# Turning the probabilities of the last attention with products instead of the transpose mode

## The reference, cut to what matters

```
s = einsum('bqghd,bkgd->bghqk', q, k) * scale
p = masked_softmax(s, mask)
o = einsum('bghqk,bkgd->bqghd', p, v)
out = g0 * o_cmp + g1 * o_slc + g2 * o_win
```

## Time and profile before

| | us |
|---|---|
| median of three timed executions | 2057.7 |
| fastest and slowest of them | 2040.02, 2061.91 |
| profiled execution, device time | 2035.77 |
| its span | 2034.0 |
| TensorE matmul busy | 1925.6 (95%) |
| VectorE busy | 1185.1 (58%) |
| ScalarE busy | 683.2 (34%) |
| last attention, first to last TensorE instruction | about 1669.7 to 1888.5 |

### The profile page before, as it was taken

The page is one execution under the profiler, slowest core; times in us unless marked ns, Lnnn a source line. Parts: engine busy times, 40 slices in busy tenths (PEclk is TensorE's granted clock), DMA queues, the critical chain, the costliest instruction groups (busy, mean ns, idle before and its releaser), DMA issues.

```text
span 2034.0 us, 25450 instructions
## 1 busy us (share of the span) xinstructions
PE 1925.6 (95%) x9553; PEld 1581.9 (78%) x9553; DVE 1185.1 (58%) x2640; ACT 683.2 (34%) x1170; POOL 101.9 (5%) x198
## 2 busy tenths in 40 slices
PE   3999999999999999989999999999999899999778
PEld 3886768988888887778888988888888776676767
DVE  5775564776476665664444487647757944533442
ACT  3323563523232342232223352323233334533121
POOL 0001110001000001100000000100110000000000
PEclk9998999999999999999999999999999999955779
DMA  8344331335334437622222243633442231010411
GB/s 333 125 145 140 100 114 63 124 126 173 138 109 127 154 125 243 221 93 104 83 90 81 79 161 128 206 128 136 135 176 83 90 118 42 1 65 1 177 39 62
DMA packets 44405, 246.05 MB, mean 121 GB/s; under 512 B 6080, under 2 KB 6304, under 8 KB 25728
## 3 DMA queue, kind: packets, MB, share of 16 engines
q1 hardware_dynamic: 23200, 153.26, 21.1%
q0 software_dynamic: 21088, 91.21, 13.4%
HBM read 229.23 MB, written 15.22 MB: 120 GB/s over the span
## 4 chain that ended last, share of the span: by engine, by line
PE 84%; DVE 9%; DMA 3%; ACT 2%; issue 1%; SPq 0%; DVEq 0%; ACTq 0%
PE ps L457 64%; PE ps L628 6%; PE ps L649 5%; PE ps L638 3%; DVE w_lo L1308 3%; DMA ada_raw<-in_ada 2%; PE ps L767 1%; ACT w_hi L923 1%; DMA bv_g<-in_bv_g 1%; DVE ada_raw L1336 1%; PE ps L879 1%; PE ps L891 1%; DVE pre L1429 1%; PE ps L714 1%; PE ps L892 0%
## 5 line engine op out<-in xcount | busy, mean ns | idle before, releaser
L1308 DVE TENSOR_TENSOR w_lo<-w_raw,w_hi 128x2048 fp32r<-128x2048 f32 x136 | 311.6, 2291 | 149.0 <-ACT w_hi L923 148.7
L923 ACT ACTIVATE w_hi<-w_raw 128x2048 fp32r<-128x2048 f32 x136 | 260.1, 1913 | 396.5 <-PE ps L457 374.0
L457 PE MATMUL ps<-h_hi,w_hi 128*128 128x512 f32 (+1 forms) x1008 | 380.9, 378 | 11.8 <-issue 4.6
L457 PE MATMUL ps<-h_lo,w_hi 128*128 128x512 f32 (+1 forms) x1008 | 375.1, 372 | 0.0
L457 PE MATMUL ps<-h_hi,w_lo 128*128 128x512 f32 (+1 forms) x1008 | 374.6, 372 | 0.0
L457 PEld LDWEIGHTS ps<-h_hi,w_hi 128*128 128x128 f32 x1008 | 192.5, 191 | 45.5 <-issue 6.2
L457 PEld LDWEIGHTS ps<-h_hi,w_lo 128*128 128x128 f32 x1008 | 192.2, 191 | 32.9
L457 PEld LDWEIGHTS ps<-h_lo,w_hi 128*128 128x128 f32 x1008 | 192.4, 191 | 30.7
L457 PE MATMUL ps<-hid_hi,w_hi 128*128 128x512 f32 (+1 forms) x576 | 211.3, 367 | 0.0
L457 PE MATMUL ps<-hid_hi,w_lo 128*128 128x512 f32 (+1 forms) x576 | 210.6, 366 | 0.0
L457 PE MATMUL ps<-hid_lo,w_hi 128*128 128x512 f32 (+1 forms) x576 | 210.5, 366 | 0.0
(11 more groups left out here) (359 smaller groups left out, 2755.5 us busy)
## 6 DMA issues: line engine op xcount, KB each, us to landing
w_raw<-in_slabs SPq DMA_DIRECT2D x136, 1024.0 KB, 4.8
ada_raw<-in_ada POOLq DMA_DIRECT2D x108, 512.0 KB, 4.5
s_tables<-s_tab POOLq DMA_DIRECT2D x4, 2692.0 KB, 9.2
s_t<-s_tables POOLq DMA_DIRECT2D x4, 2692.0 KB, 9.6
ada_first<-in_ada SPq DMA_DIRECT2D x4, 1536.0 KB, 18.3
a_bias<-in_a_bias POOLq DMA_DIRECT2D x16, 256.0 KB, 3.0
xT<-in_xT SPq DMA_DIRECT2D x1, 2048.0 KB, 20.0
s_toeplitz<-KTp POOLq DMA_DIRECT2D x32, 64.0 KB, 3.5
```

Of the source, the lines that this page charges most:

```text
L457: last = mm(o, l, r, start=start and n == 0, stop=stop and n == 2)
L923: A(w_hi[s][:], w_raw[:, s, :], ACT.Copy).then_inc(sem("hi_done"), 1)
L1308: tt(w_lo[s][:], w_raw[:, s, :], w_hi[s][:].bitcast(F32), ALU.subtract).then_inc(sem("lo_done"), 1)
```

## The change

On h_p, the last attention's probabilities, line 638 no longer uses the transpose mode: it issues an ordinary float32 product with the tile as stationary and the identity as moving operand, into the same place. The first attention keeps the transpose mode. Waits, signals, banks and order stay as they are.

```
                         for j in range(0, n, P):
                             w = min(P, n)
-                            last = nc.tensor.transpose(b[0:w, j:j + P], pt[:, u % 4, j:j + w], ident[:])
+                            if pre == "h":
+                                last = mm(b[0:w, j:j + P], pt[:, u % 4, j:j + w], ident[:], start=True, stop=True)
+                            else:
+                                last = nc.tensor.transpose(b[0:w, j:j + P], pt[:, u % 4, j:j + w], ident[:])
                         last.then_inc(sem(pre + "t_full"), 1)
```

## The result

The changed kernel took 2071.49 us (median of 4 executions, 2063.91 to 2088.23) against 2056.77 us (2040.02 to 2061.91) before. The ratio is 1.0125, with a 95% interval of 1.0072 to 1.0177: slower by 1.2%, where 2012 us was forecast. The profiled execution took 2067.79 us, with a span of 2066.0; its counterpart before had 2035.77 and 2034.0. Each later ratio is to executions of the kernel before from the same series (medians 2045.75 to 2057.16 us), and leaves out executions more than 1.5% above the fastest of their kernel, while a median holds all of them.

A forecast was written before the change was run, and what follows sets the result against it. TensorE was taken to bound the kernel, at half clock late in the last attention. With the clock held, +13.4 - 39.5 - 1.8 = -27.9 us made 2035.8 into 2007.9, plus 4 us gave 2012; range 1992 to 2062.

The forecast's parts named there:

- What bounds the stage: Last attention: the chain of waits lies on TensorE alone, 23% of it on line 638, at either clock.
- Price of a large tile: Line 638, full clock: a group's first tile costs 0.15 us more, each further tile 0.111 us.
- The lower bound: Line 638: longer turning eats its 2.2 us wait for ScalarE, leaving 0.8 us per 12 units; chance 0.06.
- Price of a small tile: Line 638, 32-key tiles: one more record of 128 columns, 0.11 us, or 0.217 at half clock.
- What the clock does: Last attention: TensorE's clock likeliest stays full to the end, on 5.6 ordinary records per us against the first attention's 4.3.
- the held case: Last attention at full clock to its end, paying 3.0 us per 12 units: 2012 us, range 1988 to 2024; chance 0.50.
- the sum: Clock held, last attention through output transposes: +13.4 - 39.5 - 1.8 = -27.9 us.
- rival 2: Last attention: the clock falls later, halfway through the 3.55 rounds, giving 2041 us; chance 0.22.
- The count: Ordinary records per us: 3.8 in the last attention, 5.6 with the change, against 4.3 in the first attention.
- The other half of my text: Last attention, counter-argument: by all records alike, 5.9 and 6.1 per us become 6.4, hardly more.
- The bridge from the profiled time to the median: Whole kernel: an earlier clock fall by two rounds explains the median's 22 us excess; holding removes the spread.

The follow-up runs named there:

- wide small tiles: Changed kernel with the 32 small tiles' stationary operand 128 columns wide instead of 32: median 2044.06 us against 2050.61; ratio 0.986 for the five fastest.
- wide scores: Kernel before, last attention's scores contracted over all 128 rows instead of 64, the other group's keys being zeros: 1969.52 us, ratio 0.961.

## Why the prediction was wrong, by its steps

**What bounds the stage: right.** TensorE is the chain before and after, and 27 of the 32 us that the span grew by are in the last attention. Of the rest 1 us came ahead of it and 4 behind it; I have not followed them up.

**Price of a large tile: right.** A first tile at full clock was to cost 0.15 us more and each further one 0.111. Measured: 0.42 against 0.26 for a group of one (1751.27 to 1751.53 before), and 1758.91 - 1757.83 = 1.08 for a group of four, 0.49 more than the 1746.47 - 1745.88 = 0.59 between the same starts before. The lower bound, that the records hide under line 638's wait for ScalarE, was not met: the difference was paid in full. By the Trainium skill (TensorE: Matmul & The Clock Gate, Terms) it would have been four times the transposition; 384 records for 192 products, at the same 0.11 us each, make it two.

**Price of a small tile: wrong.** It was put at 0.11 us, one record. It was 0.34 - 0.12 = 0.22 for itself, and 0.10 more on the products behind it: 0.32. Four of them make up nearly all of the 0.9 us that a round was dearer than forecast (3.9 instead of 3.0). The error over the stage, had the clock held, is 8 x 0.9 = 7 us. At half clock a round grew by 7.25 us instead of 6.0.

**What the clock does: wrong, and this is the failed step.** The forecast rested on "The case that I find likeliest is that it stays full to the end of the last attention", for which records per microsecond were counted. It fell at 1810. From the score of unit 65 to that of unit 95, 30 units, the changed kernel took 92.2 us; at full clock, with 23.16 - 2.33 = 20.8 us for a round without the turns (an estimate), it would have taken 52. With the drain (14.6 us) and the output transposes (3.7) at half clock the loss is 49 us, which puts the held case at about 2019 us. The four executions that held with wide small tiles, 2013 to 2021 us, agree. That is near the 2012 forecast; so the sum was about right, for a case that did not come. What came is rival 2, a later fall, with dearer rounds: by the prediction's own 16.4 us for each half-clock round, a fall at unit 64 gives 2012 + 2.7 x 16.4 = 2056, and the price that was missed (5.3 rounds at 0.9, 2.7 at 1.25) makes it about 2064, against 2067.8 in the profiled execution and 2071.5 in the median. A slip of the sum changes nothing: the upper end of the held case's own range is 2012 + 8 = 2020, not 2024.

The count was wrong in kind. It took 5.6 ordinary records per microsecond as safely above the first attention's 4.3, and a mean over 54 us as what counts. The runs show that transposes count as well, so the stage gained far less than that sum said, and that the mean over a stretch does not decide it. With the large tiles turned twice the 44 us from 1780 to 1824 had 291 records, 6.6 per us, and the clock fell; the kernel before with added products had 5.8 per us from 1800 to 1860 (350 records) and held it. And 3.5 us of further records on the small tiles, spread over the whole stage, took the clock from falling in most executions to holding in all four. The other half of my text had it: by all records alike the gain was from 6.1 to 6.4. The Trainium skill (same page, PE-mode transpose) says that a transpose does not count as busy like a matmul. The kernel with every tile turned twice disagrees: what was added to it were transposes only, and it held the clock, at 2013.5 us. That rule had made a held clock look more likely to me than it was.

**The bridge from the profiled time to the median: right in its reason.** The executions of a kernel spread as their mean clock does. The kernel before ran from 2038.23 us with a mean clock of 0.947 to 2072.42 with 0.931 in one series, and the kernels that held the clock spread over 7 to 16 us.

Left open: in which round the clock falls, which by the mean clock (0.929 to 0.951 for the kernel before) differs from one execution of the same kernel to the next; why the changed kernel's small tiles, with two records each, did not hold it; and whether rows or shorter rounds held it with wide scores.

## What to carry to other kernels

Where a stage loses its clock although TensorE is busy throughout, a mean count of records may not tell why. Look in the order of time for the part of the round where the clock falls; here it was behind the query tiles with the fewest keys, and with the large tiles as products, further records on the 32-key tiles (3.5 us in all) held it. That the sparsest part of the round decides fits these runs, but none of them filled that part alone. Test first with products that nobody reads. Adding arithmetic to hold the clock pays its own price all the time and wins only if the clock really holds: here 31 us, and in none of the four executions of the changed kernel did it hold to the end. Better is to take the standstill away, by keeping the products in one shape: with zeros in the idle rows the scores and the value products took less time, and the kernel gained 4%, held clock and shorter rounds together.

## What the runs showed of the hardware

- Among products over 128 rows, one over fewer rows costs more than its columns: a 32-column score took 0.34 us with 64 rows and 0.20 with 128, a value product 0.36 us with 32 rows and 0.17 with 128, all at full clock.
- A narrow stationary operand (32 columns) of an ordinary product costs the products behind it 0.10 us; in the transpose mode a small tile took 0.12 us and cost them nothing.
- TensorE's granted clock can fall to half with no idle stretch on the engine that the profile shows: from 1760 to 1780 in the kernel before TensorE is busy throughout, and the clock falls at 1771.
- Useless transposes made a kernel 2% faster, since they kept TensorE at 2.4 GHz: a round of 19.6 us with them against 30.4 without them at 1.2 GHz.
